# Order of four units and of one negation in a Strassen-Winograd feed-forward stage

What is changed: in a decoder layer on one core, the last four work units of each feed-forward stage run in another order, and in every unit one small copy on ScalarE stands one place earlier in the order of the weight preparation.

## The chip, the core and the metric

One core of one Trainium2 chip. The metric is the time of one execution on the device in microseconds; three runs are shown, and one more execution was profiled.

## The reference

One layer on 512 prompt rows and 8 sample rows of width 1024, all float32:

```
x += 0.5 * (silu(h @ w1) * (h @ w3)) @ w2       h = rms(x), w1, w3: 1024 x 2816, w2: 2816 x 1024      (FFN1)
x += concat(attention, gated mixing)(rms(x) @ w_in + b_in) @ w_out + b_out                          (mixer)
x += 0.5 * (silu(h @ w1) * (h @ w3)) @ w2       other weights                                       (FFN2)
x += sigmoid(rms(x) @ w_ple_gate) * (p @ w_ple_proj);  y = rms(x)
```

The change lies in FFN1 and FFN2 alone.

## The kernel before, in words

The 520 rows lie along the free dimension as two halves of 260 columns. float32 accuracy comes from three matmuls for each tile: every operand is rounded to a high part (ScalarE, a Copy to fp32r) and a low part (operand less high part), and hi*hi, hi*lo and lo*hi are added up in PSUM. Most of an FFN is computed in **units**. A unit is one 2 by 2 block product done by Winograd's form of Strassen's scheme in 7 products instead of 8: 2 blocks of 128 weight columns, the two halves of k, the two halves of the rows. An "up" unit makes a pair of hidden blocks for w1 (`("up", p, 0)`) or w3 (`("up", p, 1)`), 4 k tiles, 84 matmuls. A "dn" unit adds a chunk of hidden pairs through w2 to two of the 8 blocks of x; chunk 0 has 4 pairs (84 matmuls), chunks 1 and 2 have 3 (63 matmuls, and weights 384 instead of 512 columns wide: "short" or "narrow"). Pairs 0 and 1 are made in the standard way ahead of the units, and pair 10 (`LAST_PAIR`) goes through w2 in the standard way in 8 "down" blocks of 12 matmuls.

`UNITS` (L90 to L98) lists the units of a stage. There are 30, numbered 0 to 29 here: up pairs 2 and 3 are units 0 to 3; unit 4 is the first of pair 4, units 5 to 8 are chunk 0, unit 9 the second of pair 4, 10 to 13 pairs 5 and 6, 14 the first of pair 7, 15 to 18 chunk 1, 19 the second of pair 7, 20 to 23 pairs 8 and 9, 24 the first of pair 10, 25 and 26 half of chunk 2, 27 the second of pair 10, 28 and 29 the rest of chunk 2.

A unit's weights come in four quarters: a11 and a12 (its own tiles, loaded by SP, L759), and the pair in `w_a2` (L750, L754). SP may load `w_a2` of unit n when ScalarE has finished the preparation of unit n-2; a11 and a12 wait for the products 1 and 2 of unit n-2, which read the same cells. The raw weights, and later the low parts, share their memory. **Preparation** of a unit is a list of steps, `UNIT_STEPS` (L104):

- `w_sum13`, `w_sum24` on VectorE: sums s1 (L1502) and s3 (L1505), then s2 (L1511) and s4 (L1516). s4 reads a12 and s2.
- `w_hi_a`, `w_hi_13`, `w_hi_24` on ScalarE: rounding of a11 and a12 (L951), of s1 and s3 (L956), of s2 and s4 (L961).
- `w_neg_12` on ScalarE: minus the high part of a12 goes over raw a12 (L968); it waits until a12 was rounded and s4 made. Then POOL issues a DMA that adds the raw a12 from DRAM to it (L1292): that is a12's low part.
- `w_hi_22` on ScalarE: the same for a22 (L976, L978), and `w_lo_22` is POOL's DMA (L1300).
- `w_lo_a`, `w_lo_13`, `w_lo_24` on VectorE: low parts (L1528).

`ffn_steps` (L115) writes the order of all engines by hand. While TensorE does the products of unit n, in the order 1, 5, 4 of unit n-1, 6, 2, 3, 7, the other engines prepare unit n+1: the eleven steps are cut into five slices that stand between the products (`q`, L182). Each engine walks the same list and does its own steps, in order. Beside the preparation there are for ScalarE: a seed of a PSUM bank after product 1 (L984), "snapshots" of products 5 and 6 (L992; product 3 waits for the first, product 7 for the second), SiLU (L1000, L1003), and the rounding of h (L1009, L1015); for VectorE: the combination (`comb`, L1545 for up units and L1549 for dn, for which product 4 waits), h (L1587, L1589), its sums (L1596 to L1601) and low parts (L1608, L1614), and for dn units the additions to x (`dn_b` L1561, L1562; `dn_a` L1570; `dn_d` L1577). The work on h of a pair stands in the unit behind the pair's second up unit.

The end of a stage: unit 28, then down block 0, product 4 of unit 28, down blocks 1 to 5, unit 29 with down blocks 6 and 7. Unit 29 is prepared between the down blocks: its steps are cut into six parts (`part`, L218), part m standing behind down block m and ahead of `x_add(m)`, VectorE's addition of that block to x (L1623). Down block 3 waits for `x_add(0)` (it uses the same bank), block 4 for `x_add(1)`, block 5 for `x_add(2)`, product 1 of unit 29 for `x_add(4)`. Ahead of part 0 VectorE makes the low part of the second half of pair 10's w2 (L1427). SP's loads there, in order: the two halves of pair 10's w2 (L774), the next stage's first weights (L738), and unit 29's.

Of the kernel before, what the change touches and what calls it, by code (L numbers as in the profile page):

```python
# [36 lines left out]
KD, KF, KP = D // P, FF // P, PLE // P  # L37
# [48 lines left out]
DN_CHUNKS = ((0, 1, 2, 3), (4, 5, 6), (7, 8, 9))  # L86
LAST_PAIR = 10
LATE_SQUARES = (5, 6, 7)
H_SLOT = (2, 3, 0, 1, 2, 3, 0, 1, 2, 3, 0)
UNITS = ()  # L90
for pair_ in range(2, KF // 2):
    UNITS += (("up", pair_, 0),)
    for chunk_, pairs_ in enumerate(DN_CHUNKS):
        if pair_ == pairs_[-1] + 1:
            UNITS += tuple(("dn", chunk_, i) for i in range(KD // 2 - 2 * (pair_ == LAST_PAIR)))
    UNITS += (("up", pair_, 1),)
UNITS += tuple(("dn", len(DN_CHUNKS) - 1, i) for i in (2, 3))
UNIT_OF = {unit_: n for n, unit_ in enumerate(UNITS)}  # L98
DN_PAIRS = tuple(p for pairs_ in DN_CHUNKS for p in pairs_)
LAST_CELL = (1, 3)  # L100
N_STD = 8
N_UNIT = len(UNITS)
N_ADDED = KD // 2 * len(DN_CHUNKS)
UNIT_STEPS = ("w_sum13", "w_hi_a", "w_sum24", "w_hi_13", "w_neg_12", "w_lo_a", "w_hi_24", "w_lo_13", "w_hi_22", "w_lo_24",  # L104
              "w_lo_22")


# [7 lines left out]
def ffn_steps():  # L115
# [4 lines left out]
    def prep(i):  # L120

        kind, *arg = loads[i]
        if kind == "unit":
            return [(name, arg[0]) for name in UNIT_STEPS]
        return [("w", "up", n) for n in arg[0]]
# [14 lines left out]
    def put(n, place, *what):  # L140
        at[(n, place)] = at.get((n, place), []) + list(what)
# [23 lines left out]
    def finish(n):  # L165

        kind, p, i = UNITS[n]
        if kind == "dn":
            return [("dn_d", n)]
        return [] if i else [("silu", n)]  # L170

    for l, (kind, *arg) in enumerate(loads):
        ahead = prep(l + 1) if l + 1 < len(loads) and loads[l + 1][0] != "last" else []
        if kind == "up":
            for n in arg[0]:
                steps.append(("up", n))
                steps += side[n]
        elif kind == "unit":
            n, = arg
            is_dn = UNITS[n][0] == "dn"  # L180
            if n < N_UNIT - 2:
                q = [ahead[0:1], ahead[1:3], ahead[3:6], ahead[6:8], ahead[8:11]]  # L182
            elif n == N_UNIT - 2:
                q = [[], [], [("hi", "last", 0)], [("lo", "last", 0)], [("hi", "last", 1)]]
                put(n, "f", ("hi", "next", 0))
            else:
                q = [[("p_take", 0), ("p_take", 1), ("x_hi", 4)], [("x_lo", 0), ("x_lo", 1)],
                     [("x_hi", 5), ("x_lo", 2), ("p_split",)], [("x_lo", 3), ("x_lo", 4)],
                     [("hi", "next", 1), ("sq", 0)]]
                put(n, "f", ("sq", 1), ("sq", 2))  # L190
            behind = loads[l - 1][0] == "unit"
            steps.append(("prod", n, 1))
            if behind:
                steps.append(("comb", n - 1))
            steps += at.get((n, "a"), []) + q[0]
            steps += [("prod", n, 5), ("seed", n)] + q[1] + at.get((n, "b"), [])
            if behind:
                steps.append(("prod", n - 1, 4))
            steps += [("snap", n, 5)] + q[2] + at.get((n, "c"), []) + [("prod", n, 6)]
            if behind:  # L200
                steps += finish(n - 1)
            steps += at.get((n, "d"), []) + q[3] + [("prod", n, 2), ("snap", n, 6)] + at.get((n, "e"), []) + q[4]
            if is_dn:
                steps.append(("dn_b", n))
            steps.append(("prod", n, 3))
            if is_dn:
                steps.append(("dn_a", n))
            steps += at.get((n, "f"), []) + [("prod", n, 7)]
            if n == N_UNIT - 1:
                steps += [("down", 6), ("comb", n), ("prod", n, 4), ("sq_add", 1), ("x_lo", 5), ("x_add", 6), *finish(n)]  # L210
                steps += [("x_hi", 6), ("sq", 3), ("down", 7), ("sq_add", 2), ("x_add", 7), ("x_hi", 7), ("x_lo", 6)]
                steps += [("hi", "next", 2), ("x_lo", 7), ("p_split_lo",), ("sq", 4), ("hi", "next", 3, 1)]
                steps += [("sq_add", 3), ("sq", 5)]
                steps += [("sq_add", 4), ("sq", 6), ("sq_add", 5), ("sq", 7), ("sq_add", 6), ("sq_add", 7)]
                steps += [("lo", "next", 2), ("hi", "next", 3, 0), ("hi", "next", 4)]
        else:
            n = N_UNIT - 2
            part = [ahead[0:2], ahead[2:4], ahead[4:7], ahead[7:8], ahead[8:9], ahead[9:11]]  # L218
            for m in range(6):
                steps.append(("down", m))  # L220
                if m == 0:
                    steps += [("comb", n), ("prod", n, 4), ("lo", "last", 1)]
                steps += part[m] + [("x_add", m)]
                if m == 0:
                    steps += finish(n)
                elif m > 1:
                    steps.append(("x_hi", m - 2))
            steps.append(("p_turn",))
# [150 lines left out]
def hybrid_decoder_layer(nc, a, o):  # L379
    steps = mixer_steps()  # L380
    ffn = ffn_steps()
    done, cell, slot, free, raw, index = weight_plan(ffn)
    with ExitStack() as ctx:
# [2215 lines left out]
```

## Time and profile before

| | us |
|---|---|
| runs, median (lowest to highest) | 936.97 (936.4 to 938.34) |
| the profiled execution | 937.44, its span 935.7 |
| TensorE busy in the span | 924.1 (99%) |
| VectorE | 746.9 (80%) |
| ScalarE | 583.9 (62%) |
| POOL | 230.1 (25%) |

The granted clock is 1.0 of full speed over all of FFN1 and FFN2. In the feed-forward stages a matmul of 260 columns shows a duration of some 0.28 us, but one starts every 0.12 us, since they are pipelined: a wait of TensorE is read from the starts, not from the busy time. Durations on VectorE and ScalarE overlap a little as well; from the start of one instruction to that of the next is what one costs its engine.

### The profile page before, as it was taken

The page shows a single profiled execution, that of the slowest core. Times are in us where ns is not written, and L with a number is a line of the kernel's source. Part 1 is how long each engine was busy: PE and PEld are TensorE (multiplying, and loading weights), DVE is VectorE, ACT ScalarE, POOL GpSimd, SP SyncE. Part 2 cuts the span into 40 slices and gives each one's busy share as a digit, 9 for nine tenths or more (in the row PEclk, how much of TensorE's full clock was granted, in tenths as well). Part 3 has the DMA queues.
Part 4 walks back from the last instruction along what each step waited for, and adds up shares of the span by engine and source line. Part 5 has one row for each costly group of instructions (what it writes and reads, how often), then busy time and mean ns, then how long its engine had stood idle before and what let it go on. Part 6 is the DMA issues. An engine that isn't in the chain of part 4 may idle for free.

```text
span 935.7 us, 19675 instructions
## 1 busy us (share of the span) xinstructions
PE 924.1 (99%) x7659; PEld 912.5 (98%) x7659; DVE 746.9 (80%) x1295; ACT 583.9 (62%) x971; POOL 230.1 (25%) x179
## 2 busy tenths in 40 slices
PE   7999999999999999999999999999999999999997
PEld 7999999999999999989999999999999999999997
DVE  6979977888888787667875488997788888869786
ACT  7748755766666674656545466766567667657443
POOL 0212222223222311000318412222222232322221
PEclk9999999999999999999999999999999999999999
DMA  8958888778886779312124696888777888777912
GB/s 250 178 104 167 151 164 171 141 133 157 185 154 139 129 159 232 86 47 67 46 73 121 123 193 141 150 172 160 147 160 131 172 163 160 135 167 164 181 47 91
DMA packets 253584, 133.60 MB, mean 143 GB/s; under 512 B 15610, under 2 KB 249620, under 8 KB 253476
## 3 DMA queue, kind: packets, MB, share of 16 engines
q1 hardware_dynamic: 178020, 93.75, 36.1%
q0 software_dynamic: 75136, 37.76, 32.6%
q8 instruction: 61, 1.00, 0.4%
q10 hardware_dynamic: 336, 0.84, 0.2%
q14 instruction: 31, 0.25, 0.1%
HBM read 129.77 MB, written 3.59 MB: 143 GB/s over the span
## 4 chain that ended last, share of the span: by engine, by line
PE 94%; DVE 3%; ACT 1%; DMA 1%; issue 1%; SPq 0%; DVEq 0%
PE ps L2150 60%; PE ps L2061 25%; PE ps L2179 2%; PE ps L2095 2%; PE ps L2503 1%; PE ps L2513 1%; DMA x_rows<-in_x_prompt_dram 1%; PE ps L2368 1%; PE ps L2397 1%; DVE w_lo L1714 0%; SPq L783 0%; DVE tt L1732 0%; ACT tt L1113 0%; DVE tt L1725 0%; ACT tt L1115 0%
## 5 line engine op out<-in xcount | busy, mean ns | idle before, releaser
L2150 PE MATMUL ps<-xo_hi,w_lo 128*128 128x260 f32 x1008 | 284.7, 282 | 0.0
L2150 PE MATMUL ps<-xo_hi,w_hi 128*128 128x260 f32 x1008 | 284.5, 282 | 0.0
L2150 PE MATMUL ps<-xo_lo,w_hi 128*128 128x260 f32 x864 | 244.1, 283 | 0.0
L2150 PEld LDWEIGHTS ps<-xo_hi,w_lo 128*128 128x128 f32 x1008 | 190.1, 189 | 0.0
L2150 PEld LDWEIGHTS ps<-xo_hi,w_hi 128*128 128x128 f32 x1008 | 189.7, 188 | 0.0
L1528 DVE TENSOR_TENSOR w_lo<-w_raw,w_hi 128x512 fp32r<-128x512 f32 (+1 forms) x180 | 174.6, 984 | 15.7 <-ACT w_hi L961 7.8
L2150 PEld LDWEIGHTS ps<-xo_lo,w_hi 128*128 128x128 f32 x864 | 162.6, 188 | 0.0
L2150 PE MATMUL ps<-hop_hi,w_hi 128*128 128x260 f32 x560 | 158.9, 284 | 0.1
L2150 PE MATMUL ps<-hop_hi,w_lo 128*128 128x260 f32 x560 | 158.4, 283 | 0.0
L2150 PE MATMUL ps<-hop_lo,w_hi 128*128 128x260 f32 x560 | 158.2, 283 | 0.0
L1292 POOL DMA_DIRECT2D w_lo<-in_w_ffn_dram x60 | 76.8, 1280 | 277.3 <-ACT w_lo L968 277.3
L1300 POOL DMA_DIRECT2D w_lo<-in_w_ffn_dram x60 | 76.8, 1281 | 148.9 <-ACT w_lo L978 148.9
L984 ACT ACTIVATE ps<-ps 128x260 f32<-128x260 f32 x60 | 22.3, 372 | 143.7 <-PE ps L2150 143.7
L2150 PEld LDWEIGHTS ps<-hop_hi,w_hi 128*128 128x128 f32 x560 | 105.5, 188 | 0.9 <-issue 0.6
L2150 PEld LDWEIGHTS ps<-hop_hi,w_lo 128*128 128x128 f32 x560 | 105.5, 188 | 0.0
L2150 PEld LDWEIGHTS ps<-hop_lo,w_hi 128*128 128x128 f32 x560 | 105.3, 188 | 0.0
L951 ACT ACTIVATE w_hi<-w_raw 128x1024 fp32r<-128x1024 f32 (+1 forms) x60 | 59.9, 998 | 12.7 <-DMA w_raw<-in_w_ffn_dram 12.6
L896 ACT ACTIVATE w_hi<-w_raw 128x1024 fp32r<-128x1024 f32 x52 | 54.5, 1052 | 18.4 <-DMA w_raw<-in_w_ffn_dram 11.3
L2061 PE MATMUL ps<-xb_hi,w_hi 128*128 128x260 f32 x304 | 65.2, 295 | 0.0
L956 ACT ACTIVATE w_hi<-w_raw 128x1024 fp32r<-128x1024 f32 (+1 forms) x60 | 59.7, 995 | 3.9 <-DVE w_raw L1505 3.9
L2061 PE MATMUL ps<-xb_lo,w_hi 128*128 128x260 f32 x304 | 61.1, 282 | 0.0
L2061 PE MATMUL ps<-xb_hi,w_lo 128*128 128x260 f32 x304 | 61.1, 282 | 0.0
(365 smaller groups left out, 2045.1 us busy)
## 6 DMA issues: line engine op xcount, KB each, us to landing
w_raw<-in_w_ffn_dram SPq DMA_DIRECT2D x88, 256.0 KB, 4.4
w_lo<-in_w_ffn_dram POOLq DMA_DIRECT2D x88, 256.0 KB, 5.5
w_a<-in_w_ffn_dram SPq DMA_DIRECT2D x36, 512.0 KB, 5.7
w_raw<-in_w_ffn_dram SPq DMA_DIRECT2D x20, 512.0 KB, 6.2
w_a<-in_w_ffn_dram SPq DMA_DIRECT2D x32, 192.0 KB, 4.0
w_raw<-in_w_ffn_dram SPq DMA_DIRECT2D x32, 192.0 KB, 4.1
w_lo<-in_w_ffn_dram POOLq DMA_DIRECT2D x32, 192.0 KB, 5.3
w_raw<-in_w_in_dram SPq DMA_DIRECT2D x10, 512.0 KB, 4.5
```

The source lines that it names most:

```text
L896: nc.scalar.activation(w_at(wh, key), w_at(w_raw, key), ACT.Copy).then_inc(w_hi_ready, 1)
L951: nc.scalar.activation(w_cells(wh, s, j, "a11", 2), w_cells(w_raw, s, j, "a11", 2), ACT.Copy).then_inc(unit_hi, 1)
L956: nc.scalar.activation(w_cells(wh, s, j, "s1", 2), w_cells(w_raw, s, j, "s1", 2), ACT.Copy).then_inc(unit_hi, 1)
L984: nc.scalar.activation(ps[:, b + 1, 0:Q], ps[:, b, 0:Q], ACT.Copy).then_inc(seeded, 1)
L1292: pool.dma_start(w_cells(wl, s, j, "a12").rearrange("p o (k c) -> p (o k) c", k=k_tiles(j)), w_part(s, j, 1, 0), accum_op=ALU.add).then_in ...
L1300: pool.dma_start(w_cells(wl, s, j, "a22").rearrange("p o (k c) -> p (o k) c", k=k_tiles(j)), w_part(s, j, 1, 1), accum_op=ALU.add).then_in ...
L1528: nc.vector.tensor_tensor(w_cells(wl, s, j, name, n), w_cells(w_raw, s, j, name, n), w_cells(wh, s, j, name, n).bitcast(F32), ALU.subtract ...
L2061: ins = pe.matmul(ps[:, bank + step * h, 0:HALF], w[:, c, w0:w0 + P], m_[:, sk, h * HALF:(h + 1) * HALF], start=(first and n == 0), stop=( ...
L2095: return pe.transpose(dst, src, ident[0:n, 0:n])
L2150: ins = pe.matmul(ps[:, b, 0:Q], w[:, cc, k * P:(k + 1) * P], m_, start=(first and k == 0 and t == 0), stop=(k == kn - 1 and t == 2), skip ...
L2179: ins = pe.matmul(ps[:, bank + step * h, 0:HALF], w[:, cc, w0:w0 + P], m_[:, H_SLOT[LAST_PAIR], row, :], start=(k == 0 and n == 0), stop=( ...
L2368: ins = pe.matmul(ps[:, 4 + c, r * 2 * W:r * 2 * W + n], q_t[part, j, b * P:(b + 1) * P], k_t[part, k0:k0 + n], start=True, stop=True)
```

## The change

The condition on the chunk after pair 9 takes chunk 2 out from between the two up units of pair 10, and all four of its units follow at the end: units 24 and 25 are up, 26 to 29 are dn. The work on h of pair 10 moves with it from unit 28 to unit 26. In `UNIT_STEPS` `w_neg_12` changes places with `w_hi_13`, which holds in every unit but unit 0 of each stage, whose steps stand in a list of their own; the five slices are cut at the same places. For the preparation of unit 29 the six parts are cut anew: part 0 now has `w_sum13`, `w_hi_a`, `w_sum24`, `w_neg_12` (before: the first two), part 1 `w_hi_13` (before: `w_sum24`, `w_hi_13`), part 2 `w_lo_a`, `w_hi_24` (before also `w_neg_12`); parts 3 to 5 are as before.

```diff
     for chunk_, pairs_ in enumerate(DN_CHUNKS):
-        if pair_ == pairs_[-1] + 1:
-            UNITS += tuple(("dn", chunk_, i) for i in range(KD // 2 - 2 * (pair_ == LAST_PAIR)))
+        if pair_ == pairs_[-1] + 1 < LAST_PAIR:
+            UNITS += tuple(("dn", chunk_, i) for i in range(KD // 2))
     UNITS += (("up", pair_, 1),)
-UNITS += tuple(("dn", len(DN_CHUNKS) - 1, i) for i in (2, 3))
+UNITS += tuple(("dn", len(DN_CHUNKS) - 1, i) for i in range(KD // 2))
...
-UNIT_STEPS = ("w_sum13", "w_hi_a", "w_sum24", "w_hi_13", "w_neg_12", "w_lo_a", "w_hi_24", "w_lo_13", "w_hi_22", "w_lo_24",
+UNIT_STEPS = ("w_sum13", "w_hi_a", "w_sum24", "w_neg_12", "w_hi_13", "w_lo_a", "w_hi_24", "w_lo_13", "w_hi_22", "w_lo_24",
               "w_lo_22")
...
-            part = [ahead[0:2], ahead[2:4], ahead[4:7], ahead[7:8], ahead[8:9], ahead[9:11]]
+            part = [ahead[0:4], ahead[4:5], ahead[5:7], ahead[7:8], ahead[8:9], ahead[9:11]]
```

## Rows read from the trace of the kernel before

**Rows 1.** The page's part 1: busy us, share of the span, instructions.
```profile
PE 924.1 (99%) x7659; PEld 912.5 (98%) x7659; DVE 746.9 (80%) x1295; ACT 583.9 (62%) x971; POOL 230.1 (25%) x179
```
**Rows 2.** The chain that ended last, FFN1: start, length, what.
```profile
60.65 254.92 PE ps L2150 x2124
```
**Rows 3.** Timeline of TensorE (start, duration), units 26, 28, 29; last row FFN2's unit 28.
```profile
315.28 0.29 PE L2150 MATMUL ps<-hop_hi,w_lo 128*128 128x260 f32 x1
315.63 0.36 PE L2150 MATMUL ps<-hop_hi,w_hi 128*128 128x260 f32 x1
...
326.52 0.28 PE L2150 MATMUL ps<-hop_hi,w_hi 128*128 128x260 f32 x1
...
335.97 0.36 PE L2150 MATMUL ps<-hop_hi,w_hi 128*128 128x260 f32 x1
...
344.53 0.36 PE L2150 MATMUL ps<-hop_hi,w_hi 128*128 128x260 f32 x1
...
835.88 0.28 PE L2150 MATMUL ps<-hop_hi,w_hi 128*128 128x260 f32 x1
```
**Rows 4.** Groups by line: the negation, wide units; busy, mean ns, idle before.
```profile
L968 ACT ACTIVATE w_lo<-w_hi 128x512 fp32r<-128x512 f32 x44 | 27.4, 622 | 4.1 <-DVE w_raw L1516 3.8
```
**Rows 5.** Timelines of DVE, ACT, PE in unit 3; the snapshot at 315.11 in unit 26.
```profile
93.67 0.69 DVE L1516 TENSOR_TENSOR w_raw<-w_raw 128x512 f32<-128x512 f32 x1
...
92.99 1.06 ACT L956 ACTIVATE w_hi<-w_raw 128x1024 fp32r<-128x1024 f32 x1 [0.26 <-DVE w_raw L1505]
94.39 0.63 ACT L968 ACTIVATE w_lo<-w_hi 128x512 fp32r<-128x512 f32 x1 [0.34 <-DVE w_raw L1516]
...
96.89 0.37 ACT L992 ACTIVATE snap<-ps 128x260 f32<-128x260 f32 x1
...
315.11 0.38 ACT L992 ACTIVATE snap<-ps 128x260 f32<-128x260 f32 x1
...
97.90 0.28 PE L2150 MATMUL ps<-xo_hi,w_hi 128*128 128x260 f32 x1
```
**Rows 6.** Timeline of POOL, and the DMAs issued then with us to landing.
```profile
341.48 1.27 POOL L1292 DMA_DIRECT2D w_lo<-in_w_ffn_dram  x1 [2.89 <-ACT w_lo L968]
...
w_lo<-in_w_ffn_dram POOLq DMA_DIRECT2D x1, 192.0 KB, 5.3
```
**Rows 7.** Timeline of DVE: a narrow low part, unit 28's low part of h, its combination.
```profile
298.49 0.95 DVE L1528 TENSOR_TENSOR w_lo<-w_raw,w_hi 128x768 fp32r<-128x768 f32 x1
...
332.77 1.24 DVE L1608 TENSOR_TENSOR hop_lo<-hop,hop_hi 128x1040 fp32r<-128x1040 f32 x1 [0.62 <-ACT hop_hi L1009]
...
335.41 0.42 DVE L1549 SCALAR_TENSOR_TENSOR x<-ps,x 128x260 f32<-128x260 f32 x1
```
**Rows 8.** Timelines of DVE and ACT: preparation of unit 29; last row FFN2.
```profile
337.33 0.56 DVE L1502 TENSOR_TENSOR w_raw<-w_a 128x384 f32<-128x384 f32 x1 [0.37 <-DMA w_a<-in_w_ffn_dram]
337.99 0.56 DVE L1505 TENSOR_TENSOR w_raw<-w_a,w_raw 128x384 f32<-128x384 f32 x1
...
338.59 0.85 ACT L951 ACTIVATE w_hi<-w_raw 128x768 fp32r<-128x768 f32 x1 [1.89 <-DMA w_raw<-in_w_ffn_dram]
...
846.43 0.85 ACT L951 ACTIVATE w_hi<-w_raw 128x768 fp32r<-128x768 f32 x1 [0.37 <-DMA w_raw<-in_w_ffn_dram]
```
**Rows 9.** POOL's issue; busy by stretch (last two: DMA share, GB/s); queue in 320:324.
```profile
321.69 1.26 POOL L1292 DMA_DIRECT2D w_lo<-in_w_ffn_dram  x1 [3.46 <-ACT w_lo L968]
...
320.00:324.00 4.00, 4.00 (x35) 4.00 (x34) 3.02 (x5) 3.46 (x7) 1.26 (x1) 1.00 0.39 49
324.00:335.00 11.00, 11.00 (x94) 11.00 (x93) 5.36 (x8) 4.57 (x7) 1.27 (x1) 1.00 1.01 242
335.00:338.50 3.50, 3.50 (x30) 3.39 (x29) 3.03 (x6) 1.68 (x2) 1.49 (x1) 1.00 0.10 23
...
q0 software_dynamic: 399, 0.20, 39.4%
```
**Rows 10.** Busy by stretch: PE, PEld, DVE, ACT, POOL, clock, DMA.
```profile
61.00:99.00 38.00, 38.00 (x320) 38.00 (x319) 37.17 (x51) 29.68 (x46) 9.27 (x8) 1.00 0.77 148
```

## The prediction

> **What bounds the kernel now.** I read the page's busy times first, then the chain that ended last, then the stretches where that chain breaks, then each engine's timeline there. The first view shows TensorE busy for 924.1 of 935.7 us [rows 1]. The chain shows what that is worth: in the feed-forward stages it is one piece of matmuls after another, 2124 of them in 254.92 us, so 0.1200 us each, with no break of note between 60.65 and 315.6 [rows 2]. So the weight preparation on ScalarE and VectorE and its DMAs is hidden, nearly everywhere, and the change touches nothing but that preparation and the order of four units. It removes and adds no matmul. The only time that it can win is the little that TensorE still waits near the stages' ends, and it loses wherever a cover becomes too short.
>
> What TensorE waits for there, from starts of neighbouring matmuls less 0.12 [rows 3]. In FFN1, product 7 of unit 26 starts 0.35 after the matmul before it (0.23 lost), and its first matmul takes 0.36 instead of 0.28, 0.08 more: 0.31. Product 4 of unit 28 starts at 335.97 where 335.85 was due: 0.12 and 0.08, or 0.19 with more digits. Product 1 of unit 29, at 344.53, loses 0.21 and 0.08. In FFN2 the same places, read in the same way, lose 0.10, 0.19 and about 0.1. All of that together is 1.2 us.
>
> **The swap (negation ahead of the rounding of the sums), 58 units.** No instruction is added: ScalarE does the same two ACTIVATEs in the other order, and POOL's accumulating load of the second quarter is issued earlier, at most by the 0.95 us pitch of the rounding; POOL's order and SP's do not change. The negation needs all four sums, the rounding only two. Where ScalarE comes to them after the fourth sum, the swap is free; where it comes earlier, rounding now waits too, and all behind it on ScalarE (SiLU, the next rounding, the snapshot of product 6) is later. How often: over the run ScalarE's idle time before the negation is 4.1 us in the 44 wide units [rows 4], 0.09 each, and that is with the rounding ahead of it. I followed each unit: the end of the pair moves by 0 to 0.96 us, and the snapshot of product 6, for which product 7 waits, has more room than that everywhere but in one unit.
>
> That unit is 3 (up, pair 3, second matrix), while unit 4 is prepared. VectorE is behind, its fourth sum starts at 93.67 and takes 0.69, so ends at 94.36; the negation starts at 94.39 in either order. Now rounding ran at 92.99 in the wait; then it runs after the negation. All that follows moves by its pitch of 0.95: the snapshot of product 6 from 96.89 to 97.84, its end from 97.26 to 98.21. TensorE follows a snapshot 0.14 after its end (315.11+0.38 to 315.63 in the wait above), so product 7 starts at 98.35 instead of 97.90 [rows 5]: 0.45, and 0.08 for its slow first matmul, 0.53. FFN2 has the same times relative to the unit. Two stages: **+1.06**. Bounds: 0 if VectorE were 0.5 us earlier there, 1.1 if it is as in this execution.
>
> What the swap can win: the second quarter's low part lands earlier. The least room that I found before a product 2 is that of unit 29: issued at 341.48, landed 5.3 later at 346.8 [rows 6], wanted three products after 344.53, at 347.8. Nothing waits for it, and nothing is won.
>
> **The order of the last pair.** Before: units 24 up, 25 and 26 down, 27 up, 28 and 29 down. After: 24 and 25 up, 26 to 29 down. Unit 26 of before was a short unit (66 matmuls, 7.92 us) in which a wide one was prepared; after, no short unit prepares a wide one at this place, and its wait goes: **-0.31 and -0.10**. Four short units in a row occur already in chunk 1, with no wait in FFN1, where the chain has no break [rows 2].
>
> The h of pair 10 moves from unit 28 to unit 26. In unit 28 of before VectorE took the low part of h at 332.77, which is 6.25 after the unit's first matmul (326.52 [rows 3]), and came to the combination of the unit at 335.41, ending 335.83 [rows 7]; that was the 0.19. In unit 28 it goes: **-0.19 twice**, inside the sum of the tail below. In unit 26 it comes: the same instructions at the same offset, and one more behind the low part of h, the low part of sums 2 and 4 of unit 27, 0.95 long at a pitch of 0.87 [rows 7]. Combination done at 9.31+0.87 = 10.18, and TensorE 0.14 after it, at 10.32; product 4 of unit 26 is due two products into unit 27, at 7.92+2.15 = 10.07. 0.25 and 0.08: **+0.33 a stage, +0.66**. Bounds: 0 (ScalarE rounds h earlier) to 0.5. Unit 27's snapshot of product 6 then is just in time; I count nothing.
>
> **The tail, where both edits meet.** Offsets from unit 28's first matmul. After down block 0 VectorE does, before: low part of the last weights, sums 1 and 3 of unit 29, x_add(0), ...; after: also sums 2 and 4 ahead of x_add(0), since the negation and all that it needs stands in the first part. Down block 3 waits for x_add(0) (its bank), and is due at 13.29 (7.92 for unit 28, then 12, 9, 12 and 12 matmuls). Sum 4 needs the second quarter of unit 29. In FFN1 that lands late: VectorE waited for the other loads until 337.33 and 337.99 (10.81, 11.47) and ScalarE's rounding of the first two quarters until 338.59 (12.0) [rows 8]; a narrow sum takes 0.56, of which I count 0.47 until the next one, and 0.65 until the fourth, which reads the second. So with the landings of before, after: sum 1 at 10.81, sum 3 at 11.47, sum 2 at 11.94, sum 4 at 12.6, x_add(0) at 13.07 to 13.76, down block 3 at 13.90: 0.61 and 0.08 lost; three blocks of 1.43 on, product 1 of unit 29 at 18.27, where it was at 18.01. +0.26. In FFN2 the loads had landed by 846.43 (10.55 after the unit's start at 835.88) [rows 3, 8], x_add(0) ends near 12.4 and nothing waits: the 0.19 is won, -0.2.
>
> But the landings move. Unit 27 takes 7.9 us instead of 10.1, so the two accumulating loads of unit 28, whose first was issued at 321.69, 4.8 before unit 28, come at about -2.9 and -0.2. The DMA engines were busy 0.39 of the time from 320 to 324, 1.01 from 324 to 335, and 0.10 from there to 338.5 [rows 9]. SP's loads of that stretch (two of the last weights, the next stage's first, then four of unit 29) are released by the same matmuls as before. So one accumulating load moves from the idle stretch into the full one. In the stretch 320 to 324 POOL's queue moved 0.20 MB in 39.4% of 4.00 us [rows 9], 1.58 us of all sixteen engines, and 192 KB is 0.197 MB. The landings of unit 29 are thus later by 0 (if they find idle time) to 1.55. I take 1.2, near the upper end because the engines are full for ten microseconds, and below it because the last landings came after most engines had gone idle. FFN1: sum 1 at 12.0, sum 4 at 13.8, x_add(0) to 14.96, block 3 at 15.1, product 1 of unit 29 at 19.47: **+1.45** (0.26 to 1.8). FFN2: x_add(0) to about 13.35, 0.2 lost with the slow matmul: **0.0** (-0.2 to +0.45). Product 1 of unit 29 also waits for x_add(4); VectorE has caught up by then, so its 0.29 goes, which is within these sums. Queued behind VectorE's wait for the landing are x_add(0), dn_d and x_add(1); what waits for them is TensorE.
>
> The Trainium skill, "DMA: Bandwidth & Descriptors", section "Anatomy of one DMA", gives an accumulating queue's moving time as bytes over 436 GB/s, 0.45 us for 192 KB. The 1.58 us says otherwise [rows 9], and the measurement decides. By the page the landings would move by 0.45, the tail would be +0.7 and -0.2, and the sum 1.7.
>
> **Sum.** 1.06 - 0.41 + 0.66 + 1.45 + 0.0 = +2.76 us. The profiled execution took 937.44 (935.70 span and 1.74 around it), 0.47 above the median of the three, 936.97. The sum changes neither what lies around the span nor the rest, so I add it to the median: **939.7**.
>
> **Rivals.** A, the moved load is hidden: the landings move by under half a microsecond, since the loads run into the idle time from 335 on. For it: 0.10 busy there [rows 9]; against: the loads that matter are released by unit 28's first two products, in the full part. Time: 1.06 - 0.41 + 0.66 + 0.26 - 0.2 = 1.37, so 938.3, to 938.8 at 0.5 us. The page's price leads here as well. Chance 0.26. B, not slower: the relief alone counts. Mechanism: VectorE's fourth sum of unit 4 ends before ScalarE is through with the first quarter's rounding (decided at 93.9 or earlier, against 94.36 here), so the swap is absorbed, h of pair 10 is rounded a microsecond earlier, and the landings are not later than in FFN2. Then only the 1.2 us of waits go: 935.8. Against it: VectorE is busy 37.17 of 38.00 us from 61 to 99 [rows 10] and nothing of the change makes it earlier there. Chance 0.09. C, the last landing is held by one slow engine even longer, 1.5 us more in both stages: 2.76 + 1.5 + 1.5, 942.7. Chance 0.05. That the change doesn't do what it says is true in part already: the earlier low part is waited for by nobody.
>
> **How the numbers follow.** Forecast 0.60, A 0.26, B 0.09, C 0.05. A measurement of this kernel tells about 0.2% (1.9 us, the spread of the three runs) from no change. Over that are the forecast with its landings beyond 0.6 us, and C: slower 0.63. Within it are A and most of B, and the edge of the forecast: same 0.33. B with more than I can see: faster 0.04; all the waits that could go are worth 1.2. Range: 937.3, between A and the time of before, to 941.2, the upper bounds of all terms (936.97 + 1.1 - 0.41 + 1.0 + 1.8 + 0.45 = 940.9) and a little of C.
>
> **What would show it.** Product 7 of unit 3 some 0.45 us late in both stages behind the snapshot, with negation then rounding ahead of it. No wait at product 7 of unit 26; a short one at its product 4. VectorE idle on a DMA between the last weights' low part and x_add(0) in FFN1, and the first matmul of down block 3 over a microsecond late. If block 3 starts on time in FFN1, the tail is wrong and A holds; if product 7 of unit 3 does, the swap's price is.

## The result, and the profile after

The changed kernel takes 939.63 us (median of 15 runs, 938.32 to 941.76) where the kernel before takes 937.49 (15 runs, 936.29 to 938.39): ratio 1.0024, 95% interval 1.0018 to 1.0031, so +1.7 to +2.9 us. A second set (4 runs, 939.34 to 941.52) beside 27 runs of the kernel before gave 1.0035 (1.0021 to 1.0048). So the change makes the kernel slower, by 0.24% and 0.35%, and both intervals lie above 1. The time is the one that was forecast (939.7). The increase agrees less closely: +2.76 over a median of 936.97 was forecast, and about half a microsecond of the agreement comes from the kernel before, whose median of 15 runs is 937.49. Inside the increase one term was much too large, and others were too small or missing; they cancelled, as shown below.

The profiled execution took 938.32, the shortest of the 15; its first unit starts at 59.29, 1.2 us earlier than in the profile of before, ahead of everything that the change touches. So the two profiles are compared by stage, through TensorE's starts, and not by their ends. The granted clock over the span is nearly the same in both (0.999, before 0.998). The page's busy row of the changed kernel is nearly as before [rows 1]:

```profile
PE 923.8 (99%) x7659; PEld 912.1 (97%) x7659; DVE 747.4 (80%) x1295; ACT 585.8 (63%) x971; POOL 230.1 (25%) x179
```

Timeline of TensorE, changed kernel (start, duration, what; in brackets idle time and releaser, as the profile infers it):

```profile
96.58 0.28 PE L2150 MATMUL ps<-xo_hi,w_lo 128*128 128x260 f32 x1
97.15 0.36 PE L2150 MATMUL ps<-xo_hi,w_hi 128*128 128x260 f32 x1 [0.30 <-ACT snap L992]
...
320.40 0.28 PE L2150 MATMUL ps<-hop_hi,w_lo 128*128 128x260 f32 x1
320.75 0.36 PE L2150 MATMUL ps<-hop_hi,w_hi 128*128 128x260 f32 x1
...
325.01 0.29 PE L2150 MATMUL ps<-hop_hi,w_lo 128*128 128x260 f32 x1
325.15 0.36 PE L2150 MATMUL ps<-hop_hi,w_hi 128*128 128x260 f32 x1
...
335.62 0.39 PE L2150 MATMUL ps<-hop_hi,w_hi 128*128 128x260 f32 x1 [0.17 <-DMA w_lo<-in_w_ffn_dram]
...
339.67 0.41 PE L2179 MATMUL ps<-hop_hi,w_hi 128*128 128x260 f32 x2
...
849.35 0.35 PE L2179 MATMUL ps<-hop_hi,w_hi 128*128 128x260 f32 x1 [0.24 <-DVE x L1623]
```

The reader takes the step from one start to the next, less 0.12, and adds the 0.08 of the first matmul that shows 0.36: 0.55 at product 7 of unit 3 (and 0.54 in FFN2); 0.30 at product 4 of unit 26 (0.32 in FFN2); 0.11 at product 7 of unit 27; 0.45 at product 4 of unit 28, which waits for an accumulating load; nothing at down block 3 in FFN1 (339.67 is on time) and 0.48 in FFN2. Product 7 of unit 26 waits no more [rows 3].

Groups by line, changed kernel: the negation of wide and of narrow units (count | busy, mean ns | idle ahead of it, releaser), beside [rows 4]:

```profile
L968 ACT ACTIVATE w_lo<-w_hi 128x512 fp32r<-128x512 f32 x44 | 27.8, 631 | 13.2 <-DVE w_raw L1516 11.9
L968 ACT ACTIVATE w_lo<-w_hi 128x384 fp32r<-128x384 f32 x16 | 8.4, 524 | 5.9 <-DVE w_raw L1516 5.8
```

ScalarE now sits 13.2 us ahead of the negation in the 44 wide units instead of 4.1. Of these 9.1 us only the wait in unit 3, 1.09 in the two stages, reaches TensorE in this trace.

Every kernel was profiled once, the changed one twice. This is what TensorE lost in each profile, read as above, in us. "Undone" means that rounding stands first again in the preparation of these units; the kernels are described in the next section. A step of 1.55 ahead of product 1 of unit 29 in FFN2 is left out: it is the same in all, and TensorE has ten small matmuls of L2095 to do there (853.64 to 855.06 in the kernel before). (1 / 2 is FFN1 / FFN2; "26, 27" is products 7 and 4 of unit 26 and 7 of unit 27, both stages; "tail" is all from product 1 of unit 28 on):

```
                                unit 3   unit 18 (1 / 2)  26, 27   tail 1   tail 2    sum
before                           0        0.04 / 0.25     0.41     0.53     0.19     1.42
changed                          1.09     0.08 / 0        0.82     0.45     0.48     2.91
changed, second profile          1.09     0.45 / 1.10     0.82     0.80     0.61     4.86
swap alone                       1.07     0    / 0        0.50     0.35     0.19     2.10
order alone                      0        0    / 0        0.59     0.51     0.17     1.26
unit 4 undone                    0        0    / 0.09     0.81     0.28     0.53     1.71
x_add(0) early                   1.06     0.07 / 1.34     0.81     0.50     0.21     3.99
five undone                      0        0.10 / 0.47     0.82     0.09     1.69     3.17
swap in 2, 6, 16 alone           0        0    / 0.15     0.81     0.18     0.18     1.31
swap in 19 alone                 0        0    / 0.04     0.52     0.37     0.18     1.11
unit 28 undone                   1.09     0.21 / 0        0.63     0.93     0.81     3.66
seven undone                     0        0    / 0.19     0.62     0.96     0.21     1.97
tail and unit 4 undone           0        1.27 / 0        0.61     1.03     0.24     3.14
order alone, low part later      0        0    / 0        0        0.33     0        0.33
```

The two profiles of the changed kernel lose 1.5 and 3.4 more than that of before; the interval of the time is 1.7 to 2.9. The two stages themselves, each from the start of its first unit's first matmul to that of its last down block's last, take 590.0 us together before and 591.4 and 593.3 in the changed kernel. So in these executions TensorE's waits in the stages are the loss, and the table's columns say where.

### The profile page after: what moved, and what is told of

It is laid out like the page before. It is cut to its first block, busy times and chain, and to the rows that moved or that the text cites. A ratio compares the mean times of both kernels' runs of the same rounds, so it can differ in the third digit from the quotient of the medians.

```text
span 935.8 us, 19675 instructions
## 1 busy us (share of the span) xinstructions
PE 923.8 (99%) x7659; PEld 912.1 (97%) x7659; DVE 747.4 (80%) x1295; ACT 585.8 (63%) x971; POOL 230.1 (25%) x179
## 4 chain that ended last, share of the span: by engine, by line
PE 68%; issue 14%; DVE 9%; POOL 4%; DMA 2%; ACT 2%; DVEq 0%; ACTq 0%; POOLq 0%
PE ps L2150 35%; PE ps L2061 25%; POOL w_lo L1292 2%; PE ps L2095 2%; POOL w_lo L1300 2%; PE ps L2179 2%; DVE w_lo L1528 1%; DMA w_lo<-in_w_ffn_dram 1%; PE ps L2503 1%; PE ps L2513 1%; DMA w_raw<-in_w_ffn_dram 1%; PE ps L2368 1%; PE ps L2397 1%; DVE w_raw L1505 1%; DVE w_raw L1511 1%
## 5 line engine op out<-in xcount | busy, mean ns | idle before, releaser
L2150 PE MATMUL ps<-xo_hi,w_hi 128*128 128x260 f32 x1008 | 284.6, 282 | 0.6 <-ACT snap L992 0.6
L2150 PE MATMUL ps<-xo_hi,w_lo 128*128 128x260 f32 x1008 | 284.7, 282 | 0.0
L2150 PE MATMUL ps<-xo_lo,w_hi 128*128 128x260 f32 x864 | 244.1, 283 | 0.0
L2150 PEld LDWEIGHTS ps<-xo_hi,w_hi 128*128 128x128 f32 x1008 | 189.7, 188 | 0.9 <-DVE w_lo L1528 0.9
L2150 PEld LDWEIGHTS ps<-xo_hi,w_lo 128*128 128x128 f32 x1008 | 190.1, 189 | 0.0
L2150 PEld LDWEIGHTS ps<-xo_lo,w_hi 128*128 128x128 f32 x864 | 162.6, 188 | 0.0
L2150 PE MATMUL ps<-hop_hi,w_hi 128*128 128x260 f32 x560 | 158.8, 284 | 0.3 <-DMA w_lo<-in_w_ffn_dram 0.2
L2150 PE MATMUL ps<-hop_hi,w_lo 128*128 128x260 f32 x560 | 158.4, 283 | 0.0
L2150 PE MATMUL ps<-hop_lo,w_hi 128*128 128x260 f32 x560 | 158.2, 282 | 0.0
L2150 PEld LDWEIGHTS ps<-hop_hi,w_hi 128*128 128x128 f32 x560 | 105.5, 188 | 1.0 <-issue 0.5
L2150 PEld LDWEIGHTS ps<-hop_hi,w_lo 128*128 128x128 f32 x560 | 105.5, 188 | 0.0
L2150 PEld LDWEIGHTS ps<-hop_lo,w_hi 128*128 128x128 f32 x560 | 105.3, 188 | 0.0
L951 ACT ACTIVATE w_hi<-w_raw 128x1024 fp32r<-128x1024 f32 (+1 forms) x60 | 59.8, 996 | 6.4 <-DMA w_raw<-in_w_ffn_dram 6.4
```

What stands on the lines that cost most here:

```text
L951: nc.scalar.activation(w_cells(wh, s, j, "a11", 2), w_cells(w_raw, s, j, "a11", 2), ACT.Copy).then_inc(unit_hi, 1)
L2150: ins = pe.matmul(ps[:, b, 0:Q], w[:, cc, k * P:(k + 1) * P], m_, start=(first and k == 0 and t == 0), stop=(k == kn - 1 and t == 2), skip ...
```

## The experiments

Each is quoted with what was expected of it before it ran. Where a change in us stands beside a ratio, it and its interval are worked out from the ratio. "Undone" units come from this edit, with other numbers in the list; it holds in both stages, so one number stands for two units of the 58 (the lines behind it move by 3: L2153 is L2150, L2182 is L2179, L1626 is L1623):

```diff
-            return [(name, arg[0]) for name in UNIT_STEPS]
+            names = list(UNIT_STEPS)
+            if arg[0] in (2, 4, 6, 16, 19):
+                names[3:5] = names[4], names[3]
+            return [(name, arg[0]) for name in names]
```

**The swap alone**, in the kernel before:

```diff
-UNIT_STEPS = ("w_sum13", "w_hi_a", "w_sum24", "w_hi_13", "w_neg_12", ...
+UNIT_STEPS = ("w_sum13", "w_hi_a", "w_sum24", "w_neg_12", "w_hi_13", ...
```

> Only the swap, in all units; the order of the units and the cut of the tail as before. Theory 1 (the loss is a sum of short waits, the largest being product 7 of unit 3 behind the snapshot of product 6): +0.54 in each stage, so about +1.1 us less the 0.25 of product 7 of unit 18 in FFN2, 938.3 where before has 937.5, and product 7 of unit 3 late in both stages as in the changed kernel. Rival 1 (the swap is hidden and the loss lies in the last units, whose order moves loads into a full stretch): 937.5, no wait at unit 3 that matters.

939.01 (11 runs, 937.42 to 941.24) beside 936.41: 1.0022 (1.0013 to 1.0031), +1.2 to +2.9. The wait at unit 3 is there. Timeline of ScalarE in this kernel:

```profile
94.36 0.63 ACT L968 ACTIVATE w_lo<-w_hi 128x512 fp32r<-128x512 f32 x1 [1.66 <-DVE w_raw L1516]
94.90 1.05 ACT L956 ACTIVATE w_hi<-w_raw 128x1024 fp32r<-128x1024 f32 x1
...
97.81 0.37 ACT L992 ACTIVATE snap<-ps 128x260 f32<-128x260 f32 x1
```

Timeline of TensorE, the first matmul of product 7:

```profile
98.33 0.36 PE L2150 MATMUL ps<-xo_hi,w_hi 128*128 128x260 f32 x1 [0.29 <-ACT snap L992]
```

The negation waits 1.66 for the fourth sum, with the rounding now behind it; the snapshot is at 97.81, where it was at 96.89 [rows 5]. But the time rose by more than the 1.07 of this wait; its runs fall into two groups, 937.42 to 937.93 (5) and 939.01 to 939.66 (5) with one above, and the profile is of the lower. Theory 1 has the unit right, not the whole amount.

**The order alone**: the changed kernel with the old `UNIT_STEPS` and the old cut of `part`.

> Only the new order of the last pair's units; rounding ahead of negation and the cut of the tail as before. Theory 1: no wait at product 7 of unit 3; product 4 of unit 26 late by 0.3 in both stages, product 7 of unit 27 by 0.1, against waits that go (0.41 at unit 26, some at 28 and 29): within 0.4 us of before plus what the landings of unit 29 cost, 937.3 to 938.3. Rival 1: the whole loss, 939.6. If the swap and the order alone add up to the whole change, the two do not meet; if they fall short of it, what is missing is in the tail, where both meet.

936.75 (11 runs) beside 936.41: 1.0005 (0.9997 to 1.0014). As theory 1 expected; rival 1, by which the order carries the whole loss, falls. The order gives 0.41 at product 7 of unit 26 and takes 0.59 at its product 4.

By the times the two edits add up: +2.1 (1.2 to 2.9) for the swap and +0.5 (-0.3 to +1.3) for the order, where the whole change has +2.2 (1.7 to 2.9). So the times show no meeting of the two that could be measured, and most of the loss comes with the swap (the changed kernel's second set has +3.3, 2.0 to 4.5). By the traces it is otherwise: the swap alone loses 0.7 more than before and the order alone 0.2 less, the whole change 1.5 and 3.4 more. One place of a meeting shows below, at product 4 of unit 28; how much of the time it makes is not shown.

**Unit 4 undone**: the list is (4,).

> The whole change, but in the preparation of unit 4 alone (which runs during unit 3) the rounding of the sums stays ahead of the negation, as before. Theory 1: product 7 of unit 3 is on time again in both stages and 1.1 us come back against the whole change: 938.5 against 939.6. Rival 1: the wait is only moved, another product of unit 3 or 4 is late instead, and the time stays at 939.6. Bound by the trace: 0 to 1.2 us.

939.03 (9 runs, 936.43 to 941.59): 1.0026 (1.0015 to 1.0037). The wait at unit 3 is gone from the trace. The shortest run is 0.8 above the shortest of the kernel before beside it (935.59); for the changed kernel that difference is 2.0 (938.32 and 936.29). But the ratio did not fall below the changed kernel's 1.0024 and 1.0035. The intervals leave room for about 1 us and for nothing, so the price of unit 3 is shown by the traces, with and without it, and not by the time. Something else was costing too.

**x_add(0) early**: the changed kernel with the old cut, x_add(0) ahead of sums 2 and 4.

> The whole change, but in the last phase x_add(0) stands ahead of sums 2 and 4 of unit 29 again, as before. Theory 1: down block 3 no longer waits for x_add(0) (0.48 in FFN2 of the changed kernel's profile, 0 in FFN1): -0.5 us in that execution, up to -1.5 where the landings are late in FFN1 too, and up to 0.3 given back at product 1 of unit 29: 938.4 to 939.4. Rival 2 (the typical execution is longer than the profiled one for the landings of unit 29, which hold x_add(0)): 938.0 and a smaller spread of the runs. If the time stays at 939.6, the order of x_add(0) and the sums costs nothing.

939.15 (6 runs): 1.0031 (1.002 to 1.0042). Down block 3 is on time in both stages, as expected (the tail of FFN2 is 0.21), and the time did not fall: +2.9 (1.9 to 3.9) over the kernel before, where theory 1 expected +0.9 to +1.9. The profiled execution was a long one, 941.75, and shows a wait that no theory had: 1.34 at product 7 of unit 18 in FFN2. That led to the next four.

**Five undone**, as in the diff above.

> The whole change, but with the rounding of the sums ahead of the negation again in the preparation of units 2, 4, 6, 16 and 19 (that is during units 1, 3, 5, 15 and 18), the places where the swap left the snapshot of product 6 the least room before product 7 (0.24, 0.14, 0.33, 0.41 and 0.16 to 0.43 us in the traces; 0.14 is a wait). Theory 2 (the swap costs 1.1 us at unit 3, and the rest of its price in executions where a load lands late and the thin room of the other four no longer covers it): the time of the order alone plus 0.2 for units 27 and 28, 936.9 to 937.3 where before has 936.4, and few runs above 938.5. Rival 2 (the rest comes from somewhere else that the swap touches, for instance the accumulating loads that are issued earlier everywhere): no better than with unit 4 alone undone, 938.5 to 939.0, runs above 939 as often as there.

938.15 (11 runs): 1.0013 (1.0004 to 1.0021), between the two expectations.

**Swap in units 2, 6 and 16 alone**, in the kernel before.

> The kernel before, with negation ahead of rounding in the preparation of units 2, 6 and 16 alone (during units 1, 5 and 15), not in that of unit 4. Theory 2: the lowest runs as before (935.6 to 936.2), since 0.1 to 0.27 us of room is left in an execution without late loads, but more runs 1 to 3 us above them: median 0.3 to 1.5 above before. Rival 2: 936.4, as before, with the same spread.

936.87 (11 runs, 935.45 to 937.76) beside 937.05: 0.9996 (0.9987 to 1.0004). Theory 2 expected +0.3 to +1.5, and the interval ends at +0.4, so all but its lowest end falls here: the room before product 7 shrank (unit 1: 0.91 to 0.24), but it cost nothing that can be measured.

**Swap in unit 19 alone**, in the kernel before.

> The kernel before, with negation ahead of rounding in the preparation of unit 19 alone (during unit 18), where one trace of a long execution (with x_add(0) early) shows product 7 of unit 18 in FFN2 1.34 us late behind a load that took 5.5 us instead of 3.8. If it is the swap at this place that makes it late: lowest runs as before, some 1 to 2 us above, median up to +1. If the late load does it in either order (the trace shows rounding of the first quarter waiting for it, ahead of both): 936.4, as before.

937.46 (11 runs): 1.0 (0.9991 to 1.0009). The swap at that place costs nothing that can be measured (under 0.9 us either way).

**The changed kernel once more.**

> The changed kernel once more, beside the three others on one chip and with a second profile. All theories: +2.2 to +2.7 us over before. Theory 2: if the profiled execution is one of the long ones, its trace shows a late load with a wait of 0.3 to 2 us at product 7 of unit 1, 5, 15 or 18, beside the 0.54 of unit 3, which stays the same. Rival 2: the additional time is spread or lies at other places, or before the first unit.

940.36 (4 runs): 1.0035 (1.0021 to 1.0048). Its profile (941.52) is of a long execution, with the late load. Timeline of ScalarE in FFN2's unit 18:

```profile
747.45 1.06 ACT L951 ACTIVATE w_hi<-w_raw 128x1024 fp32r<-128x1024 f32 x1 [1.68 <-DMA w_raw<-in_w_ffn_dram]
748.42 0.37 ACT L992 ACTIVATE snap<-ps 128x260 f32<-128x260 f32 x1
748.68 0.62 ACT L968 ACTIVATE w_lo<-w_hi 128x512 fp32r<-128x512 f32 x1
749.20 1.05 ACT L956 ACTIVATE w_hi<-w_raw 128x1024 fp32r<-128x1024 f32 x1
750.15 1.04 ACT L961 ACTIVATE w_hi<-w_raw 128x1024 fp32r<-128x1024 f32 x1
751.10 0.37 ACT L992 ACTIVATE snap<-ps 128x260 f32<-128x260 f32 x1
```

Timeline of TensorE, the same kernel and place:

```profile
750.49 0.28 PE L2150 MATMUL ps<-hop_hi,w_lo 128*128 128x260 f32 x1
751.62 0.36 PE L2150 MATMUL ps<-hop_hi,w_hi 128*128 128x260 f32 x1 [0.84 <-DVE w_lo L1528]
```

The load's row among the DMA issues of that stretch (KB, us to landing):

```profile
w_raw<-in_w_ffn_dram SPq DMA_DIRECT2D x1, 256.0 KB, 5.2
```

The rounding of the first quarter (L951) waits for a12 of unit 19; behind it ScalarE works without a gap, 3.65 us to the snapshot, and product 7 follows the snapshot by the same 0.14 as at unit 3 (751.10 + 0.37 + 0.14 is 751.61; the bracket names VectorE's low part, which only happens to end about then). Neither order of the two steps could make this shorter: the wait is settled ahead of both.

**Unit 28 undone**: the list is (28,).

> The whole change, but with rounding ahead of negation again in the preparation of unit 28 alone (during unit 27). Theory 3 (the two edits meet in the last units: the order puts the second accumulating load of unit 28 into the full stretch, and the swap issues it 0.75 later on top, 7.90 after the start of unit 27 against 7.15): the load is issued near 7.15 and lands before product 4 of unit 28 wants it, so the 0.32 to 0.45 of FFN1 go, and product 7 of unit 27 no longer waits its 0.1; down block 3 stays late by 0.3 to 0.6, since nothing there changes. -0.5 to -0.7 us against the whole change, some +1.7 against before. Rival 3 (the DMA engines are full, and an earlier issue lands no earlier): product 4 of unit 28 is as late as in the changed kernel. The verdict is by the trace; the time can hardly tell it.

940.0 (12 runs): 1.0026 (1.0016 to 1.0035). POOL's second accumulating load of unit 28 in the changed kernel, by the timeline and by the DMA issues (KB, us to landing):

```profile
326.27 1.27 POOL L1300 DMA_DIRECT2D w_lo<-in_w_ffn_dram  x1 [1.45 <-ACT w_lo L978]
```

```profile
w_lo<-in_w_ffn_dram POOLq DMA_DIRECT2D x1, 192.0 KB, 9.3
```

The same two views of this kernel:

```profile
326.12 1.27 POOL L1303 DMA_DIRECT2D w_lo<-in_w_ffn_dram  x1 [0.71 <-ACT w_lo L981]
```

```profile
w_lo<-in_w_ffn_dram POOLq DMA_DIRECT2D x1, 192.0 KB, 7.0
```

Counted from the start of unit 27 the issue moves from 7.90 to 7.19 and the landing from 17.21 to 14.23 in FFN1 (16.16 to 15.59 in FFN2); product 4 of unit 28 is on time, as theory 3 expected. It brought nothing that the time shows: down block 3, due 0.4 earlier then, is 0.93 late instead of 0. Timelines of VectorE and of TensorE in this kernel:

```profile
337.47 0.56 DVE L1505 TENSOR_TENSOR w_raw<-w_a 128x384 f32<-128x384 f32 x1 [1.38 <-DMA w_a<-in_w_ffn_dram]
...
339.24 0.56 DVE L1519 TENSOR_TENSOR w_raw<-w_raw 128x384 f32<-128x384 f32 x1
339.72 0.70 DVE L1626 SCALAR_TENSOR_TENSOR x<-ps,x 128x520 f32<-128x520 f32 x1
```

```profile
340.56 0.48 PE L2182 MATMUL ps<-hop_hi,w_hi 128*128 128x260 f32 x2 [0.69 <-DVE x L1626]
```

VectorE idles 1.38 on unit 29's loads with x_add(0) behind all four sums. The two waits of the tail lie one after the other: who removes the first meets the second.

**Seven undone**: the list is (2, 4, 6, 16, 19, 28, 29), and the old cut.

> The new order, with negation ahead of rounding in 51 of 58 units: rounding is ahead again in the preparation of units 2, 4, 6, 16, 19, 28 and 29, and the last phase has the cut of before. Theory 3 (what the swap costs beside unit 3 and the thin places is its meeting with the order in the last units; in the other 51 units it is free): +0.2 to +0.5 us over before, as the order alone had (+0.3), 1 us below the kernel with five units undone. Rival 3 (the swap costs something in all units): +1.1, as with five undone.

937.34 (12 runs) beside 936.9: 1.0002 (0.9992 to 1.0011). The seven numbers stand for 14 units, so negation is first in 44 of the 58 here and not in 51, as the expectation has it. In these 44 it costs nothing that can be measured; rival 3's +1.1 lies just outside the interval, which ends at +1.0. Against five undone 1.0 us came back, which points at the tail, but 0.11% between two ratios with half-widths of 0.09% is not shown.

**Tail and unit 4 undone**: the list is (4, 28, 29), and the old cut; the last open point on theory 2.

> The new order with negation ahead of rounding in 55 of 58 units: rounding is ahead in the preparation of units 4, 28 and 29 alone, and the last phase has the cut of before. It differs from the kernel with seven undone by units 2, 6, 16 and 19. Theory 3 (the swap costs at unit 3 and in the last units, and the wait at product 7 of unit 18 is the landing of the last load less 2.15, in either order): as with seven undone, +0.2 to +0.5 us over before. Theory 2 (the thin rooms of units 1, 5, 15 and 18 cost in many executions, when the order is new too): +1.0 to +1.5, as the difference between one and five units undone (2.4 and 1.2 over before) suggests.

937.4 (11 runs) beside 936.99: 1.0005 (0.9991 to 1.0018). The middle is what theory 3 expected, and next to that of seven undone. But the interval, -0.8 to +1.7, holds theory 2's +1.0 to +1.5 as well, so that units 2, 6, 16 and 19 cost nothing with the new order is likely and not shown. (Negation is first in 52 units here, not in 55.) Its profile happens to show 1.27 at unit 18 in FFN1, with the load landing in 5.4 us.

**Order alone, low part of h later**: the order alone, and

```diff
-            put(n + 1, "e", ("h_hi", p), ("h_lo", p))
+            put(n + 1, "e", ("h_hi", p))
+            put(n + 3, "b", ("h_lo", p))
```

> Meant to beat both kernels: the new order alone (rounding first everywhere, the cut of before), and the low part of h of pair 10 taken in unit 28 after the combination of unit 27 instead of in unit 26 ahead of the combination of unit 26. Theory: product 4 of unit 26 no longer waits (0.29 in each stage with the order alone), nothing else becomes late, since down block 0 wants that low part only at the end of unit 28: -0.6 against the order alone, -0.3 against before. Rival: the low part now delays VectorE in unit 28 and product 4 of unit 28 waits instead, as it did before the change (0.19 a stage): 0 to +0.1 against before.

936.47 (12 runs, 935.36 to 938.14) beside 936.9: 0.9993 (0.9985 to 1.0002). The trace is as expected: no wait at unit 26, 27 or at product 4 of unit 28, 0.33 us lost in all instead of 1.42. VectorE's timeline in unit 28 of this kernel (its lines are 1 further on):

```profile
325.75 0.43 DVE L1550 SCALAR_TENSOR_TENSOR x<-ps,x 128x260 f32<-128x260 f32 x1 [0.37 <-PE ps L2151]
326.09 1.23 DVE L1609 TENSOR_TENSOR hop_lo<-hop,hop_hi 128x1040 fp32r<-128x1040 f32 x1
329.00 0.43 DVE L1578 SCALAR_TENSOR_TENSOR x<-ps,x 128x260 f32<-128x260 f32 x1 [1.67 <-PE ps L2151]
```

The low part (1.23) stands where VectorE was idle anyway. This beats the changed kernel clearly, its interval ends below the other's; that it beats the kernel before is likely and not shown, since the interval holds 1.

## Why the prediction was right, and where it was not

**Swap at unit 3: right.** +1.06 forecast, 1.09 in both profiles of the changed kernel, gone with unit 4 undone. Product 7 at 97.15 is 0.14 behind the snapshot's end, as was reckoned. Timeline of ScalarE, changed kernel:

```profile
96.64 0.37 ACT L992 ACTIVATE snap<-ps 128x260 f32<-128x260 f32 x1
```

**Unit 26: right.** -0.41 for its product 7, and +0.66 for its product 4 (0.61 in the first profile, 0.61 in the second). The last experiment, which moves the low part of h alone, takes all of it away.

**Unit 27's snapshot "just in time; I count nothing": wrong by 0.2.** It waits 0.11 and 0.10. It was called just in time without a room being worked out. In this unit the negation waits for the fourth sum, and the snapshot is later for it; with unit 28 undone the wait is gone. Timeline of ScalarE, changed kernel:

```profile
322.74 0.53 ACT L968 ACTIVATE w_lo<-w_hi 128x384 fp32r<-128x384 f32 x1 [1.36 <-DVE w_raw L1516]
323.17 0.83 ACT L956 ACTIVATE w_hi<-w_raw 128x768 fp32r<-128x768 f32 x1
323.91 0.83 ACT L961 ACTIVATE w_hi<-w_raw 128x768 fp32r<-128x768 f32 x1
324.64 0.37 ACT L992 ACTIVATE snap<-ps 128x260 f32<-128x260 f32 x1
```

**The tail in FFN1: the step that failed, +1.45 forecast, -0.1 and +0.3 measured** (0.45 and 0.80 less the 0.53 of before). The chain of waits was the right one. In nine of the ten passes that have the new cut (a pass is one stage of one profile; five profiles have this cut), block 3 starts 1.83 to 1.90 after a12 of unit 29 lands, and the forecast had 1.9, 15.1 for a landing at 13.2. The term that was mis-sized is the landing: 13.2 forecast, 11.33 and 11.73 measured in FFN1 of the changed kernel, counted from the start of unit 28. In the tenth pass, the first profile's FFN1, block 3 waits for nothing, since product 4 of unit 28 had waited ahead of it. VectorE is done with x_add(0) at 339.41 there, and block 3 starts at 339.67; timeline of VectorE, changed kernel:

```profile
338.24 0.56 DVE L1516 TENSOR_TENSOR w_raw<-w_raw 128x384 f32<-128x384 f32 x1
338.72 0.69 DVE L1623 SCALAR_TENSOR_TENSOR x<-ps,x 128x520 f32<-128x520 f32 x1
```

The step of the prediction was "with the landings of before" plus 1.2. The landings of before in FFN1 were one draw, and a late one: a12 of unit 29 landed 11.99 after the start of unit 28 there, and 11.12, 10.39 and 11.40 in the three other kernels with the old order. With the new order (nine profiles, the last experiment left out) it lands at 11.04 to 12.14, mean 11.51: 0.3 over the mean of the old order (11.23; a rough figure, with four values that spread over 1.6), and 0.5 ahead of the one row that I built on. In FFN2 it is 10.10 to 10.67 in the old order (mean 10.42) and 11.49 to 12.64 in the new one (mean 11.73): +1.3, and I had taken 1.2. The prediction's other value for this step, an estimate of 0.45 us for 192 KB from the figure of the Trainium skill, "DMA: Bandwidth & Descriptors", section "Anatomy of one DMA", would have been near in FFN1 and not in FFN2. (With it the prediction's terms add up to 1.8, not to the 1.7 that it gives.) By the prediction's own sign, block 3 on time in FFN1 means that rival A holds. It is on time in the first profile and 0.47 late in the second; and A's condition, landings that move by under half a microsecond, is met by the mean of FFN1 and not by that of FFN2.

**The tail in FFN2: 0.0 forecast, +0.3 and +0.4 measured.** The mechanism was the right one, x_add(0) behind sums that wait for the landing: it was forecast to end near 13.35 and ends at 13.18 (timeline of VectorE, changed kernel, unit 28 starting at 836.02):

```profile
846.23 0.56 DVE L1502 TENSOR_TENSOR w_raw<-w_a 128x384 f32<-128x384 f32 x1 [0.90 <-DMA w_a<-in_w_ffn_dram]
...
848.04 0.56 DVE L1516 TENSOR_TENSOR w_raw<-w_raw 128x384 f32<-128x384 f32 x1
848.51 0.69 DVE L1623 SCALAR_TENSOR_TENSOR x<-ps,x 128x520 f32<-128x520 f32 x1
```

But block 3 was due at 12.92, not at 13.29. Unit 28 holds product 4 of unit 27. Before, unit 27 is an up unit and that product has 12 matmuls; in the changed kernel it is a narrow dn unit with 9. So 63 matmuls, 7.55 us, lie between the first matmul of unit 28 and down block 0, where the kernel before has 66, 7.92. The prediction kept the 7.92 of before: 0.37. (Unit 27 of the kernel before takes 9.73, not the 10.1 that the prediction gives; nothing hangs on that.)

**Product 4 of unit 28: "-0.19 twice" was wrong in FFN1.** VectorE's part went as forecast. The accumulating load that moved into the full stretch came late itself, in 9.3 us instead of 6.2 before; the prediction priced what the moved load does to others, and not what the others do to it. It is a meeting of both edits: the order puts it there, the swap issues it 0.75 later (7.90 against 7.15 with the order alone), since ScalarE reaches it behind a negation that waited. It is not bound to FFN1: with five undone the same load lands later still in FFN2, 9.9 us after its issue, and product 4 of unit 28 waits 1.0 there.

**Unit 18: not in the sum.** The prediction listed where TensorE waits near the stages' ends. Over the 28 passes of the 14 profiles (one stage of one profile each) that wait is the landing of a12 of unit 19 less 2.15 us after the start of unit 18, to within 0.02 (landing at 2.41: 0.25 in the kernel before; 2.59: 0.45; 3.24: 1.10; 3.42: 1.27; 3.49: 1.34; at 2.0 and below: nothing), in either order of the steps. SP issues it at -1.98 in all of them, and it lands in 3.1 to 5.5 us. Where units 17 and 18 are prepared with the negation first, 5 of 18 passes landed behind 2.5; where not, none of 10 (2.41 at most). That fits the second group of runs of the swap alone, but it is not shown: these passes are few, and the two kernels with the tail undone have the same steps there and measure +0.2 and +0.5. Why the swap alone costs 1.2 to 2.9, when its trace has 0.7 more than before, stays open to that extent; the swap in units 17 and 18 alone, or in unit 4 alone, was not run.

So that the forecast time came out is luck in good part: +1.45 that was too much by 1.2 to 1.5, against 0.2 at unit 27, 0.3 to 0.4 in FFN2's tail and, by the execution, -0.2 to +1.2 at unit 18. Rival B, by which the swap is absorbed at unit 3, is refuted by the trace; rival A's 1.37 over before is near the short execution (1.5), and below the interval (from 1.7). Rival C's 942.7 came in none of the 19 runs (941.76 at most).

## What to carry to other kernels

Exchange two steps on an engine only where the one that comes first has its inputs already: idle time of that engine (13.2 us ahead of the negation) says little; the room before the one consumer that has least says more (1.09 of it reached TensorE by the trace). Two edits can meet: price the last units with both in place, the load that is moved as well as the loads that it moves into, and expect the next wait in line when the first is taken away. Where a step rests on a landing, take it from several passes and both stages of a trace, not from one row. Where the order of units changes, count the matmuls of the neighbours anew.

## What the runs showed of the hardware that was not expected

The same accumulating load of 192 KB, unit 28's second, took 5.8 us to land in FFN1 when issued 1.38 ahead of unit 28's first matmul (order alone with the low part later), 6.2 when 2.46 ahead (the kernel before), 7.0 when 0.65 ahead (unit 28 undone) and 9.3 when 0.04 ahead (the changed kernel). The stretch that follows is the one in which the DMA engines were busy 1.01 of the time before [rows 9], with SP's loads under way. Between the last two kernels 0.7 us of issue were worth 3.0 of landing in FFN1 and 0.6 in FFN2. Over all passes of the new order with these two times of issue the means are 2.4 in FFN1 (five late passes against three early ones) and 1.3 in FFN2 (five against four). And a plain load of 256 KB that is issued at the same offset in every pass lands in 3.1 to 5.5 us: that spread alone, at a place with no room for it, makes 1.10 us between the two profiles of the changed kernel, and up to 1.34 in a pass.
